# Opening of a three-block kernel: row statistics by pairs of row tiles, modulation sums shared by VectorE and TensorE, weight tiles split on GpSimd

## The reference, cut to what matters

```
c_act = silu(c)                                   # c: 1024 numbers
mod = c_act @ ada_w[l] + ada_b[l]                 # 1024 -> 3 x 1024
shift, scale, gate = jnp.split(mod[:, None, :], 3, axis=-1)
u = _rmsnorm(h, norm_g[l]) * (1.0 + scale) + shift
proj = u @ w_in[l]                                # 1024x1024 @ 1024x7168
```

## Time and profile before

| | us |
|---|---|
| median of 3 runs | 2764.65 (2763.58 to 2766.03) |
| profiled execution, first to last instruction (span) | 2763.9 |
| TensorE busy | 2689.4 (97%) |
| VectorE busy | 2086.6 (75%) |
| opening, to the barrier | 67.7 |

### The profile page before, as it was taken

How to read it: one execution, slowest core, us unless ns; L and a number is a source line. 1 busy time by engine, 2 the same in 40 slices (tenths; PEclk the granted TensorE clock), 3 DMA queues, 4 the chain that set the end, 5 groups by cost and what they waited for, 6 DMA issues and landing times.

```text
span 2763.9 us, 33573 instructions
## 1 busy us (share of the span) xinstructions
PE 2689.4 (97%) x13192; PEld 2199.6 (80%) x13192; DVE 2086.6 (75%) x2796; ACT 1069.2 (39%) x1599; POOL 477.0 (17%) x254
## 2 busy tenths in 40 slices
PE   6999999999999999999999999999999999999998
PEld 5888888888888878778875678888887888888887
DVE  6999998873724663369998886688186988887978
ACT  5111112243413332245537751365232554555332
POOL 0000000000100002001210001354211656655000
PEclk8999999999999999999999999999999999999999
DMA  5312222224325452011101032100132222225431
GB/s 223 116 63 69 94 97 61 84 92 142 99 107 175 136 176 90 31 62 39 47 30 36 32 123 96 46 31 23 62 115 80 96 77 89 87 77 188 170 99 61
DMA packets 97710, 250.18 MB, mean 91 GB/s; under 512 B 7361, under 2 KB 34369, under 8 KB 96018
## 3 DMA queue, kind: packets, MB, share of 16 engines
q1 hardware_dynamic: 93010, 231.49, 24.4%
q10 hardware_dynamic: 4288, 15.73, 1.5%
q0 software_dynamic: 256, 0.82, 0.1%
HBM read 202.92 MB, written 45.09 MB: 90 GB/s over the span
## 4 chain that ended last, share of the span: by engine, by line
PE 80%; DVE 14%; issue 2%; ACT 1%; DMA 1%; DVEq 0%; ACTq 0%
PE pair L370 16%; PE pair L372 16%; PE pair L371 16%; PE pair L3657 7%; PE pair L3242 5%; PE pair L3244 5%; PE pair L3245 5%; DVE counted L1942 3%; PE pair L2593 2%; DVE reached L1993 1%; PE pair L2156 1%; DVE top_i L1999 1%; PE pair L1754 1%; PE pair L2172 1%; PE pair L2185 1%
## 5 line engine op out<-in xcount | busy, mean ns | idle before, releaser
L370 PE MATMUL pair<-u_hi,w_hi 128*128 128x512 f32 x768 | 302.1, 393 | 1.2 <-PEq L92 0.9
L641 DVE SCALAR_TENSOR_TENSOR conv_acc<-aT,cols,conv_acc 128x1024 f32<-128x1024 f32 x232 | 297.9, 1284 | 6.7
L371 PE MATMUL pair<-u_lo,w_hi 128*128 128x512 f32 x768 | 300.3, 391 | 0.0
L372 PE MATMUL pair<-u_hi,w_lo 128*128 128x512 f32 x768 | 300.3, 391 | 0.0
L370 PEld LDWEIGHTS pair<-u_hi,w_hi 128*128 128x128 f32 x768 | 145.2, 189 | 32.7 <-issue 2.4
L371 PEld LDWEIGHTS pair<-u_lo,w_hi 128*128 128x128 f32 x768 | 145.0, 189 | 30.6 <-issue 0.7
L372 PEld LDWEIGHTS pair<-u_hi,w_lo 128*128 128x128 f32 x768 | 145.0, 189 | 30.6
L370 PE MATMUL pair<-h_hi,ch_hi 128*128 128x512 f32 x392 | 153.8, 392 | 2.8 <-ACT ch L1824 2.6
L372 PE MATMUL pair<-h_hi,ch_lo 128*128 128x512 f32 x392 | 152.7, 389 | 0.0
L371 PE MATMUL pair<-h_lo,ch_hi 128*128 128x512 f32 x392 | 152.6, 389 | 0.0
L1014 POOL TENSOR_TENSOR yrT<-yrT,gate_c 128x1024 f32<-128x1024 f32 x8 | 18.9, 2366 | 758.1 <-ACT yrT L907 758.1
(11 more groups left out here) (510 smaller groups left out, 7105.1 us busy)
## 6 DMA issues: line engine op xcount, KB each, us to landing
wt<-in_w_ch SPq DMA_DIRECT2D x60, 512.0 KB, 3.4
wo_raw<-in_w_out SPq DMA_DIRECT2D x44, 512.0 KB, 3.6
wt<-in_w_up SPq DMA_DIRECT2D x10, 1024.0 KB, 4.9
w_raw<-in_w_up SPq DMA_DIRECT2D x10, 1024.0 KB, 4.8
g_spill<-g_stage SPq DMA_DIRECT2D x40, 256.0 KB, 2.2
ada_mod<-in_ada_mod SPq DMA_DIRECT2D x4, 2048.0 KB, 14.3
wt<-in_w_conv SPq DMA_DIRECT2D x16, 512.0 KB, 3.5
qk<-qk_st SPq DMA_DIRECT2D x8, 1024.0 KB, 6.4
```

The costliest lines, as they stand in the source:

```text
L370: nc.tensor.matmul(bank, w[0], x[0], start=(first and k == 0), stop=False)
L371: nc.tensor.matmul(bank, w[0], x[1], start=False, stop=False)
L372: return nc.tensor.matmul(bank, w[1], x[0], start=False, stop=(last and k == n_k - 1))
L641: nc.vector.scalar_tensor_tensor(dst, x, w, conv_acc[:], ALU.mult, ALU.add).then_inc(conv_step, 1)
```

## The change

- Row statistics by pairs of row tiles: DVE squares tiles 0, 1, 3, 5, 7 and ACT 2, 4, 6; `deviation(q)` and `inverse(q)` each handle two row tiles. GpSimd scales tiles 5 and 7, DVE the others.
- The copies to `xT` are shared: ACT 0, 1, 2, 4, 6, DVE 3, 5, 7.
- Each modulation block is loaded in two halves of 1 MB. Block 2 moves to memory of its own and is loaded without a wait; block 3 waits for four transposed tiles in place of eight.
- DVE sums none of block 0's slices, four of block 1's and five of blocks 2 and 3 (`DVE_SHARE`); TensorE does the others by one-column matmuls: 32 for block 0, 20 for block 1, 16 each for blocks 2 and 3, where it had 8 each.
- GpSimd makes both parts of weight tiles 0 and 1.

The removed lines of the scalar, vector and tensor parts stand in the functions printed above and are left out here.

```diff
@@ -136,8 +136,8 @@
-        ada_mod = [at(kb, f"ada_mod{j}", [P, KT, HALF]) for j, kb in enumerate((52, 68, 85, 101))]
-        ada_sum = [at(kb, f"ada_sum{j}", [P, HALF]) for j, kb in enumerate((181, 183, 201, 203))]
+        ada_mod = [at(kb, f"ada_mod{j}", [P, KT, HALF]) for j, kb in enumerate((52, 68, 133, 85))]
+        sum_dve = {j: at(kb, f"sum_dve{j}", [P, HALF]) for j, kb in ((1, 181), (2, 183), (3, 201))}
@@ -147,11 +147,12 @@
+        ada_in = [[sem(f"ada_in{j}{half}") for half in "ab"] for j in range(N_MOD)]
@@ -159,15 +160,24 @@
+        DVE_SHARE = (range(0), range(0, 4), range(0, 5), range(0, 5))
...
+        DVE_TILES, POOL_TILES = (0, 1, 2, 3, 4, 6), (5, 7)
+        ACT_COPIES, DVE_COPIES = (0, 1, 2, 4, 6), (3, 5, 7)
...
         def x_quarter(q):
...
+        def x_turned(t):
+            return (xT[:, :, t * P:(t + 1) * P],
+                    flat(pair[XT_PAIR[t % 3]]).rearrange("p (k s) -> p k s", s=P))
         def open_sync(sp):
             def modulation(j):
-                sp.dma_start(ada_mod[j][:], a["ada_mod"][j, :, :].rearrange("p (k c) -> p k c", k=KT))\
-                    .then_inc(ada_in[j], 16)
+                src = a["ada_mod"][j, :, :].rearrange("p (k c) -> p k c", k=KT)
+                for half in range(2):
+                    ks = slice(half * KT // 2, (half + 1) * KT // 2)
+                    sp.dma_start(ada_mod[j][:, ks, :], src[:, ks, :]).then_inc(ada_in[j][half], 16)
@@ -177,8 +187,8 @@
             modulation(0)
             first_tiles(sp, a["w_conv"], 0, glu_w)
             modulation(1)
-            sp.wait_ge(xt_mm, TT)
             modulation(2)
+            sp.wait_ge(xt_mm, 4)
             modulation(3)
             for n in (2, 3):
@@ -189,12 +199,18 @@
...
+            def deviation(q):
+                if q:
+                    act.wait_ge(sq_act, q)
+                act.wait_ge(sq_dve, q + 2)
...
+                nc.scalar.activation(rstd[:, 2 * q:2 * q + 2], ss[:, 2 * q:2 * q + 2], ACT.Sqrt, bias=eps6[:],
...
+            def copy(t):
+                act.wait_ge(xt_mm, t + 1)
+                to, src = x_turned(t)
+                nc.scalar.activation(to, src, ACT.Copy).then_inc(xt_act, 1)
...
             def modulated(k):
@@ -208,50 +224,44 @@
...
+            deviation(0)
+            square(2)
+            deviation(1)
+            square(4)
+            deviation(2)
+            copy(0)
+            square(6)
+            deviation(3)
+            for t in ACT_COPIES[1:]:
+                copy(t)
+            act.wait_ge(xt_act, len(ACT_COPIES))
+            act.wait_ge(xt_dve, len(DVE_COPIES))
+            for k in range(KT):
...
         def open_vector(dve):
...
             def square(t):
...
+            def inverse(q):
+                dve.wait_ge(std_done, q + 1)
+                r = rstd[:, 2 * q:2 * q + 2]
+                nc.vector.reciprocal(r, r).then_inc(inv_set, 1)
+            def normalize(t):
+                dve.wait_ge(inv_set, t // 2 + 1)
+                dve.wait_ge(x_in[t // 2], 16)
+                nc.vector.tensor_scalar(x_sb[:, t, :], x_sb[:, t, :], rstd[:, t:t + 1], None, ALU.mult).then_inc(xn_dve, 1)
+            def copy(t):
+                dve.wait_ge(xt_mm, t + 1)
+                to, src = x_turned(t)
+                nc.vector.tensor_copy(to, src).then_inc(xt_dve, 1)
...
             def shift_and_scale(j):
@@ -265,67 +275,122 @@
+            def modulation(j):
+                to = sum_dve[j][:]
+                for done, k in enumerate(DVE_SHARE[j]):
+                    dve.wait_ge(ada_in[j][k // 4], 16)
+                    x, c = ada_mod[j][:, k, :], cact[:, k:k + 1]
+                    if done == 0:
+                        nc.vector.tensor_scalar(to, x, c, None, ALU.mult).then_inc(step_dve[j], 1)
+                        continue
+                    dve.wait_ge(step_dve[j], done)
+                    nc.vector.scalar_tensor_tensor(to, x, c, to, ALU.mult, ALU.add).then_inc(step_dve[j], 1)
...
+            square(0)
+            square(1)
+            inverse(0)
...
+            square(3)
+            square(5)
+            inverse(1)
+            normalize(2)
+            normalize(3)
+            inverse(2)
+            normalize(4)
+            square(7)
+            inverse(3)
+            normalize(6)
+            for t in DVE_COPIES:
+                copy(t)
...
+            modulation(1)
+            low(0)
+            shift_and_scale(1)
+            low(1)
+            for j in range(2, N_MOD):
+                modulation(j)
+                low(2 * j - 2)
+                shift_and_scale(j)
+                low(2 * j - 1)
+            low(KT - 2)
+            low(KT - 1)
...
+        def open_gpsimd(pool):
+            def normalize(t):
+                pool.wait_ge(inv_set, t // 2 + 1)
+                pool.wait_ge(x_in[t // 2], 16)
+                nc.gpsimd.tensor_scalar(x_sb[:, t, :], x_sb[:, t, :], rstd[:, t:t + 1], None, ALU.mult).then_inc(xn_pool, 1)
+            def weight_parts(n):
+                pool.wait_ge(glu_w[n], 16)
+                nc.gpsimd.tensor_tensor(w_parts[0][:, n, :, :], wt[:, n, :, :],
+                                        ones_col[:].rearrange("p (a b) -> p a b", b=1).broadcast_to([P, KT, P]),
+                                        ALU.mult).then_inc(job_hi, 1)
+                pool.wait_ge(job_hi, n + 1)
+                nc.gpsimd.tensor_tensor(w_parts[1][:, n, :, :], wt[:, n, :, :], w_parts[0][:, n, :, :].bitcast(F32),
+                                        ALU.subtract).then_inc(job_lo, 1)
+            for t in POOL_TILES:
+                normalize(t)
+            pool.wait_ge(eps_set, 1)
+            for n in range(2):
+                weight_parts(n)
...
         def open_tensor(pe):
...
             for t in range(TT):
...
+                if t in DVE_TILES:
+                    pe.wait_ge(xn_dve, DVE_TILES.index(t) + 1)
+                else:
+                    pe.wait_ge(xn_pool, POOL_TILES.index(t) + 1)
...
+                    if t - 3 in ACT_COPIES:
+                        pe.wait_ge(xt_act, ACT_COPIES.index(t - 3) + 1)
+                    else:
+                        pe.wait_ge(xt_dve, DVE_COPIES.index(t - 3) + 1)
...
             def modulation(j):
...
+                for half in range(2):
+                    pe.wait_ge(ada_in[j][half], 16)
...
+                summed = len(DVE_SHARE[j])
...
+                    to = mod_sum[:, j, i:i + 1]
+                    for k in range(summed, KT):
+                        last = nc.tensor.matmul(to, ada_mod[j][:, k, i * P:(i + 1) * P], cact[:, k:k + 1],
+                                                start=(k == summed), stop=(not summed and k == KT - 1))
+                    if summed:
+                        if i == 0:
+                            pe.wait_ge(step_dve[j], summed)
+                        last = nc.tensor.matmul(to, sum_dve[j][:, i * P:(i + 1) * P], ones_col[:], start=False, stop=True)
...
             modulation(0)
...
+            modulation(1)
+            for j in range(N_MOD - 1):
+                for k in (2 * j, 2 * j + 1):
+                    for n in range(2):
...
+                if j + 2 < N_MOD:
+                    modulation(j + 2)
+            for n in range(2):
+                for k in (KT - 2, KT - 1):
+                    tile_step(pe, n, k)
...
         def load_tiles(sp, src, first, n, ready, used, base):
@@ -480,6 +545,10 @@
             def _(dve):
...
+            @block.gpsimd
+            def _(pool):
+                open_gpsimd(pool)
```

More of the change, by code:

```diff
@@ L210, in open_scalar @@
             nc.scalar.activation(cact[:], col("c"), ACT.Silu).then_inc(cact_ok, 1)
-            for half, tiles in enumerate(((0, 2), (4, 6, 7))):
-                for t in tiles:
-                    square(t)
-                deviation(half)
-            for t in range(TT):
-                act.wait_ge(xt_mm, t + 1)
-                nc.scalar.activation(xT[:, :, t * P:(t + 1) * P],
-                                     flat(pair[XT_PAIR[t % 3]]).rearrange("p (k s) -> p k s", s=P),
-                                     ACT.Copy).then_inc(xt_ok, 1)
-            high_part(act, 0)
-            act.wait_ge(xt_ok, TT)
-            modulated(0)
-            high_part(act, 1)
-            for k in range(1, KT):
+            deviation(0)
[11 more added lines that the diff above has]
+            for k in range(KT):
                 modulated(k)
@@ L229, in open_vector @@
             chain = Count(dve, dve1)
-            steps = [0] * N_MOD
             def square(t):
@@ L304, in modulation @@
             def modulation(j):
-                pe.wait_ge(ada_in[j], 16)
+                for half in range(2):
+                    pe.wait_ge(ada_in[j][half], 16)
                 pe.wait_ge(cact_ok, 1)
```

63 lines of the change are left out of this document (6 added, 57 removed).

## The result

| | before | after |
|---|---|---|
| median of four runs, measured side by side | 2764.76 (2763.58 to 2766.03) | 2781.59 (2779.33 to 2784.09) |
| profiled execution, span | 2763.9 | 2777.5 |
| first transpose / transposes end | 14.63 / 24.5 | 10.34 / 23.3 |
| last one-column matmul of block 0 ends | 26.8 | 35.1 |
| first product / opening's last product ends | 36.42 / 66.7 | 45.47 / 81.0 |

The end of the opening's last product is taken as in the prediction, as its start plus one step of 0.23.

A forecast was written before the change was run, and what follows sets the result against it. TensorE, busy 97% of the span, was taken as the bound. First product at 42.3 plus 34.7 us ends the opening at 77.0 against 66.7, +10.3 us, so a median of 2775.0, range 2767 to 2781.

The forecast's parts named there:

- First transpose: Start of TensorE's transposes in the opening: at about 10.1, 4.5 us earlier than before, through the new statistics.
- Tile 4: Its transposes need ACT's copy of tile 1, which stands behind the last root: copy done at 18.0.
- Transposes: End of the transposes in the opening: 21.6 if the clock has come up, so 2.9 of 4.5 us are left.
- Either end is hidden: GpSimd's scaling takes 0.69 to 2.38 us, taken as 1.9; tile 7's runs from 17.3 and is wanted at 20.7.
- Block 0: Its 32 one-column matmuls on TensorE: 15 at the high clock, 17 at the low, 10.4 us, ending at 32.0.
- u_hi to first product: From u_hi at 32.5, DVE's four block 1 slices to 35.4, then 16 slow one-column matmuls: first product at 42.3.
- First product to the end: Products, sums of blocks 2 and 3, and a clock fall in each of these blocks: 34.7 us, ending at 77.0.
- A microsecond in the opening should stay: TensorE works without a gap after the opening, so a microsecond gained or lost there carries to the end.
- Rival 1: One-column matmuls without a gap keep the clock up: 2761.7, or 2763.5 with one fall; chance 0.14.
- Rival 2: GpSimd holds DVE up in the opening, up to 4.8 us on top: 2780; chance 0.06.
- Rival 3: The transposes stay at the low clock and end at 24.8: 2781.5; chance 0.04.

The follow-up runs named there:

- e1: The changed kernel, but VectorE scales all row tiles, so GpSimd only splits the weight tiles; median +15.6 us against before, ratio 1.0055.
- e3: The kernel before with only the new shares (VectorE sums 0, 4, 5 and 5 slices); median +18.8 us, ratio 1.0061.
- e4: The changed kernel with an extra 512-column float32 matmul behind every four one-column matmuls, 20 in all; median +23.4 us against before, ratio 1.0084.
- e15: The changed kernel with two and three extra 512-column matmuls in TensorE's stops at 1157 and 1388; median +13.3 us against before, ratio 1.0047.
- e8: The kernel before with nine extra dense 512-column matmuls where TensorE waits in the opening; median +0.3 us, ratio 1.0001.
- e10: The kernel before with 32 more products behind the opening's last, results unused; median +12.5 us, ratio 1.0044.
- e2: The changed kernel, but VectorE sums seven of eight slices of every modulation block as before; median +11.8 us against before, ratio 1.0038.

## Why the prediction was wrong

*First transpose*, 10.1: 10.34. *Tile 4*, 18.0: 18.11. Right, with the reason given (the copy of tile 1 stands behind the last root, and this behind the fifth square).

*Transposes*, 21.6: 23.3, with block 0 beginning at 23.1. This step failed, by the duration of a GpSimd scaling. I bounded it by 0.69 and 2.38 from other operations and took 1.9; the two took 4.45 and 2.84, the second with only one copy of VectorE beside it. I had tile 7's start at 17.3; it stood behind tile 5's in GpSimd's queue until 19.3. "Either end is hidden" was true of my ends only. e1 without them ends at 21.9. Why the first took 4.45 is open: VectorE's scalings and square ran beside it, but no run took them away.

*Block 0*, 10.4 us: 12.0. The mechanism is right (one-column matmuls don't keep the clock up; e3 and e4 show it from both sides), its size was off: I took 3.1 us at the high level, it was 1.9, in e1 3.3, in e15 4.1. It can't be read from one trace to better than 2 us.

*u_hi to first product*, 9.8: 9.8. *First product to the end*, 34.7: 35.5; falls at blocks 2 and 3 as forecast, but the one at block 2 lasted 6.8 us, which is 3.4 lost where I took 2.05.

So the opening is +14.3 where 10.3 was forecast: 1.5 from the transposes, 1.6 from block 0, 0.8 behind the first product. The first of these has a cause that e1 shows. The other two are the clock, and e15, the same opening with +10.9, was within 0.6 of the forecast; how near an execution comes to the sum is in part luck.

*"A microsecond in the opening should stay"*, and nothing should differ after the barrier: false. Behind the barrier the traces differ from before's by -1.2 to +6.5 us, and e8, with a shorter opening, lost nearly as much as e10 with a later one. With the opening's +14.3 alone the median would have been 2779.0, inside the range. The other 2.5 us of the 16.8 stay open: the changed kernel's own trace has -0.7 behind the barrier, its other executions have no trace, and 14.3 lies within the interval of 13.3 to 20.7. What such differences consist of the traces show (longer waits of TensorE at a few places, and falls of the clock of 1.7 us behind some of them). What decides in which execution they come stays open, and so does whether filling the stops gains anything in the median.

*Rivals.* Rival 1 (clock up) is refuted by after and e3. Rival 2 (GpSimd holds DVE) is not what happened here, though e2 shows the price when it does; GpSimd was slow itself. Rival 3's end (2781.5) is the measured median by luck: the transposes were fast from tile 2 on (in e15's trace 3.52 us for the first 16, 1.97 for the next), and block 0 began at the high clock.

## What to carry to other kernels

One-column matmuls cost half at the high clock (0.21 against 0.43 us here), and the long rows of them in the changed kernel lost it or had it fall right behind: price them at the low one. Bound an operation that the trace doesn't show by its own kind on its own engine, and if there is none, let the upper bound be wide and ask what it would cost there. In a kernel whose TensorE is 97% busy, a stop of 2 us can cost 1.7 us more in some executions, as the ones at 1157 and 1388 did; 0.1% between two kernels may be just that, whatever was gained at the start. A trace shows which execution you have, so compare what lies behind the edited stage inside one execution before you explain a median by it.
